# Even heads: block transposes and the value branch inside the inverse; odd heads: a split state update and an earlier product

## The chip, the cores and the metric

One core of one Trainium2 chip runs one program for the whole inference step. The metric is the device time of one execution in microseconds (us); lower is better. The kernel before has 1951.6 us as the median of three runs.

## The reference

One step of a two-layer decoder trunk over 512 prompt tokens and 8 x 8 sample tokens, model width 1024, all in float32. The two layers differ in their mixer; each is followed by a SwiGLU feed-forward block.

```python
def run_trunk(x, conv_a_prev, conv_qkv_prev, delta_prev, ret_prev, pos, w):
...
        h = rmsnorm(x, w['norm_mix'][i])
        if i % 2 == 0:
            y, ca, cq, s = even_mixer(...)   # short conv + gated delta rule, 4 heads of 128
        else:
            y, r = odd_mixer(...)            # retention, 8 heads, qk 128, v 256
        x = x + y.astype(x.dtype)
        h = rmsnorm(x, w['norm_ffn'][i])
        f = (jax.nn.silu(h @ w['ffn_w_gate'][i]) * (h @ w['ffn_w_up'][i])) @ w['ffn_w_down'][i]
        x = x + f.astype(x.dtype)
...
# even mixer, per head
    a_mat = jnp.eye(c, dtype=F32) + jnp.einsum('bnhid,bnhjd->bnhij', kb, kc) * decay * strict
    u_base = lax.linalg.triangular_solve(a_mat, vb, left_side=True, lower=True, unit_diagonal=True)
...
# odd mixer, per head: the state kept for the samples
        r = r * cdec + jnp.einsum('bhck,bhcv->bhkv', k_ * kdec, v_)
```

## The kernel before

All activations live in SBUF transposed (features on the 128 partitions, 512 + 64 = 576 tokens along the free axis). Every weight product is a **unit**: a 128-column slice of a weight over all 1024 rows, 512 KB, loaded by SyncE (`load`, L426) into one of four `raw` slots, split by ScalarE into a high part (`split_hi`, L440) and by GpSimd, in four instructions, into a low part (`split_lo`, L449, instructions at L455), and multiplied on TensorE as high x high, high x low and low x high (`unit`, L466; 48 matmuls of 288 columns). A load waits until the unit three before it has been split, a split until the unit two before it has been multiplied. Two PSUM accumulators alternate; `mx`, four PSUM banks, is for the small products of a head. Each engine runs its own hand-ordered program; numbered steps on one semaphore per engine (`Steps`, tables `E_*` and `O_*`) tie them together.

**Even heads** (three in a loop, a fourth written out). TensorE (`even_tensor`, L1492) puts pieces of units between the small products. In order: unit 0, the norm of k (l2k), three quarters of unit 1, k times k (kk), the norm of q (l2q), the rest of unit 1, the transposes of k (tk), k times q (kq), the transposes of v (tv), P1, and then for s = 2, 4, ..., 64 two eighths of a unit, P_s (`level_p`, L1521), two eighths of a unit, Q_s (`level_q`, L1536). These levels invert the unit triangular 128 x 128 matrices of the four chunks by doubling the size of the inverted diagonal blocks. The inverse `zi` and its transpose `xi` are both kept: P_s is the masked matrix times zi; ScalarE copies it to `pp` (`copy_p`, L1090); Q_s consists of xi times pp (bank 2) and pp times xi (bank 3), with two 64 x 64 products for the samples at s <= 4; VectorE subtracts both banks from zi (z_s) and xi (x_s) (`inverse_step`, L1341). P_(2s) waits for x_s, which VectorE does after z_s. After P64 and Q64 comes the recurrence over the four chunks (u0, S0, ...), on TensorE still mixed with eighths of the next head's k and q units.

VectorE (`even_vector`, L1252) does the four-tap convolutions of k, q and v (`conv_qkv`, L1260), in that order, before it scales k to kT; later vb, the beta-scaled v, straight after the copy kd. During levels 16 to 32 it does the gated convolution of the first mixer (L1357 to L1371). ScalarE (`even_scalar`, L1082) has silu of k, q and v, the squares, the inverse norms (Ln then Exp), and table loads between the silu set and the Ln/Exp set. GpSimd makes the masks b_s and scaled copies.

**Odd heads** (seven in a loop, an eighth written out). Units 0 to 3 are values and gates, 4 and 5 the next head's k and q; then `rows_unit` (L494) multiplies the head's output by two units of the output weight, eight products that each `add_to_x` (L594) adds to x. Near the end TensorE does the variance sums, the last eighth of unit 4, `kvs` (eight states' updates into all four banks of `mx`), unit 5, the rows units. VectorE updates the eight 128 x 256 states `r_s` in one instruction (step rs, L862) once kvs is done, before the first add; between the adds it turns the next head's k and q (`turn_step`, L783). SyncE, at the end of a head's loads, waits for rs and loads the next head's decay constants `ch` (`head_decays`, L1018); then come the next head's units 0 and 1, a wait until ScalarE's DMAs of r_s have ended, the load of the next r_s, unit 2 and so on. ScalarE waits for rs before it sends r_s out and splits the next head's unit 0.

## Time and profile before

| | us |
|---|---|
| median of three runs | 1951.6 |
| lowest and highest of them | 1938.78, 1952.1 |
| the profiled execution's own time | 1946.06 |
| its span, first to last instruction | 1944.3 |
| TensorE busy in the span | 1840.1 |
| mean granted TensorE clock | 0.977 |

The profile is of one execution. Matmuls are pipelined, so that busy time of TensorE is no measure of its peak; the times at which its instructions start, and what they waited for, are what is read below. A granted clock of 1.0 is 2.4 GHz, 0.5 is 1.2 GHz. "x10" means that ten like instructions are merged in a row; a bracket tells how long the engine was idle before the row and what released it.

### The profile page before, as it was taken

The numbers are of one execution on the slowest core, as the hardware profiler recorded it, in microseconds if no ns is written. First come the engines' busy times: TensorE is split into PE (matmuls) and PEld (weight loads), VectorE is DVE, ScalarE is ACT, GpSimd is POOL, SyncE is SP. The second block draws the span as 40 slices with busy tenths as digits, with TensorE's granted clock in tenths as the row PEclk, the third lists the DMA queues.
The fourth block names the chain that finished last, engine by engine and source line by source line (L and its number), as shares of the span: only waits on it lengthen the run. The fifth ranks groups of instructions, "written<-read, shape, count | busy, mean of one in ns | idle before, by whom it ended". The sixth has DMA issues, their size and how long they took to land.

```text
span 1944.3 us, 33917 instructions
## 1 busy us (share of the span) xinstructions
PE 1840.1 (95%) x13431; PEld 1768.5 (91%) x13431; DVE 589.2 (30%) x883; ACT 618.9 (32%) x846; POOL 850.3 (44%) x1061
## 2 busy tenths in 40 slices
PE   6899998998899999999899999999987999999997
PEld 5898888987799999999899999999986999999996
DVE  2636354444311111000452354245425111111002
ACT  3625243342322222112433243334334222222112
POOL 2534435343545445446533443344334444544443
PEclk9999999998999999999899999999998999999998
DMA  5112121211222222223331432243231222222221
GB/s 147 44 34 77 34 75 43 69 42 34 59 86 76 86 78 84 79 78 91 93 106 52 136 115 86 72 125 115 76 94 57 78 84 86 76 86 75 85 81 57
DMA packets 254285, 153.24 MB, mean 79 GB/s; under 512 B 5136, under 2 KB 246549, under 8 KB 254240
## 3 DMA queue, kind: packets, MB, share of 16 engines
q1 hardware_dynamic: 239582, 139.85, 25.1%
q10 hardware_dynamic: 14658, 12.79, 2.0%
q8 instruction: 29, 0.48, 0.1%
q14 instruction: 16, 0.13, 0.0%
HBM read 138.26 MB, written 14.36 MB: 78 GB/s over the span
## 4 chain that ended last, share of the span: by engine, by line
PE 62%; issue 17%; POOL 10%; DVE 6%; ACT 3%; DMA 1%; DVEq 0%; POOLq 0%; ACTq 0%; SPq 0%
PE acc L463 46%; POOL w_lo L455 9%; PE acc L483 7%; PE mx L1494 6%; DVE n_xf L585 1%; PE mx L526 1%; DVE ca L1267 1%; PE mx L875 1%; DMA x_in<-in_x_sample 1%; PE acc L1649 0%; ACT L534 0%; DVE qT L1316 0%; POOL xn_lo L569 0%; ACT std L1085 0%; DVE yT L585 0%
## 5 line engine op out<-in xcount | busy, mean ns | idle before, releaser
L455 POOL TENSOR_TENSOR w_lo<-raw,w_hi 128x256 fp32r<-128x256 f32 x932 | 712.1, 795 | 972.8 <-ACT w_hi L447 972.8
L463 PE MATMUL acc<-xn_hi,w_hi 128*128 128x288 f32 x2224 | 497.8, 305 | 7.6 <-POOL w_lo L455 6.3
L463 PE MATMUL acc<-xn_hi,w_lo 128*128 128x288 f32 x2224 | 477.5, 296 | 0.0
L463 PE MATMUL acc<-xn_lo,w_hi 128*128 128x288 f32 x2224 | 476.4, 296 | 0.0
L447 ACT ACTIVATE w_hi<-raw 128x1024 fp32r<-128x1024 f32 (+1 forms) x237 | 246.9, 1043 | 523.2 <-PE acc L463 475.8
L463 PEld LDWEIGHTS acc<-xn_hi,w_hi 128*128 128x128 f32 x2224 | 357.9, 189 | 23.4 <-issue 16.4
L463 PEld LDWEIGHTS acc<-xn_lo,w_hi 128*128 128x128 f32 x2224 | 359.0, 189 | 0.0
L463 PEld LDWEIGHTS acc<-xn_hi,w_lo 128*128 128x128 f32 x2224 | 358.6, 189 | 0.0
L599 DVE TENSOR_TENSOR x<-acc,x 128x576 f32<-128x576 f32 (+1 forms) x112 | 84.7, 756 | 314.7 <-PE acc L463 312.5
L691 DVE TENSOR_TENSOR f_h<-acc,f_g 128x576 f32<-128x576 f32 x44 | 33.3, 758 | 444.8 <-PE acc L463 444.8
L463 PE MATMUL acc<-h_lo,w_hi 128*128 128x288 f32 x704 | 150.8, 295 | 0.0
L463 PE MATMUL acc<-h_hi,w_hi 128*128 128x288 f32 x704 | 150.8, 295 | 0.0
L463 PE MATMUL acc<-h_hi,w_lo 128*128 128x288 f32 x704 | 150.7, 295 | 0.0
L463 PEld LDWEIGHTS acc<-h_lo,w_hi 128*128 128x128 f32 x704 | 113.7, 188 | 0.0
L463 PEld LDWEIGHTS acc<-h_hi,w_hi 128*128 128x128 f32 x704 | 113.7, 188 | 0.0
L463 PEld LDWEIGHTS acc<-h_hi,w_lo 128*128 128x128 f32 x704 | 113.7, 188 | 0.0
L483 PE MATMUL acc<-xn_hi,w_hi 128*128 128x288 f32 x416 | 92.9, 306 | 13.0 <-ACT xn_hi L555 13.0
L483 PE MATMUL acc<-xn_lo,w_hi 128*128 128x288 f32 x416 | 93.8, 308 | 6.5 <-POOL xn_lo L569 5.5
L658 ACT ACTIVATE f_g<-acc 128x576 f32<-128x576 f32 x44 | 28.7, 651 | 202.8 <-PE acc L463 105.6
L483 PE MATMUL acc<-xn_hi,w_lo 128*128 128x288 f32 x416 | 92.4, 305 | 0.0
L483 PEld LDWEIGHTS acc<-xn_hi,w_hi 128*128 128x128 f32 x416 | 70.1, 198 | 14.7 <-issue 14.7
L483 PEld LDWEIGHTS acc<-xn_lo,w_hi 128*128 128x128 f32 x416 | 69.4, 196 | 10.5 <-POOL xn_lo L569 8.1
(325 smaller groups left out, 2179.6 us busy)
## 6 DMA issues: line engine op xcount, KB each, us to landing
raw<-in_odd_w_in SPq DMA_DIRECT2D x48, 512.0 KB, 4.0
raw<-in_ffn_w_gate SPq DMA_DIRECT2D x44, 512.0 KB, 3.7
raw<-in_ffn_w_up SPq DMA_DIRECT2D x44, 512.0 KB, 3.8
raw<-in_ffn_w_down SPq DMA_DIRECT2D x32, 512.0 KB, 3.7
raw<-in_even_w_in SPq DMA_DIRECT2D x29, 512.0 KB, 3.9
r_s<-in_state_ret SPq DMA_DIRECT2D x8, 1024.0 KB, 6.3
raw<-in_odd_w_out SPq DMA_DIRECT2D x16, 512.0 KB, 3.7
out<-r_s ACTq DMA_DIRECT2D x8, 1024.0 KB, 6.0
```

The costliest lines, as they stand in the source:

```text
L447: nc.scalar.activation(w_hi[:, d, 0:n * P], raw[:, s, 0:n * P], ACT.Copy).then_inc(hi_ready, 1)
L455: ins = nc.gpsimd.tensor_tensor(w_lo[:, d, piece], raw[:, s, piece], w_hi[:, d, piece].bitcast(F32), ALU.subtract)
L463: ins = nc.tensor.matmul(out, w, mv[:, tokens], start=first and n == 0, stop=last and n == 2)
L483: ins = nc.tensor.matmul(out, w, mv[:, k, tokens], start=k == 0 and n == 0, stop=k == KT - 1 and n == 2)
L526: ins = nc.tensor.matmul(mx[:, h, 0:HALF], ones, n_sq[:, t % 2, h * HALF:(h + 1) * HALF], start=t == 0, stop=t == KT - 1)
L585: nc.vector.scalar_tensor_tensor(out=dst, in0=x[:, t, :], scalar=g, in1=n_rs[:, :], op0=ALU.mult, op1=ALU.mult).then_inc(y_norm if last el ...
L599: nc.vector.tensor_tensor(dst, pair_view(p), dst, ALU.add).then_inc(drained[p], 1)
L658: nc.scalar.activation(f_g[:, :], pair_view(0), ACT.Silu).then_inc(drained[0], 1)
L691: nc.vector.tensor_tensor(f_h[:, :], pair_view(1), f_g[:, :], ALU.mult).then_inc(drained[1], 1)
L875: return nc.tensor.matmul(out, lhs, rhs, start=start, stop=stop)
L1267: step(nc.vector.scalar_tensor_tensor(out=b[:, 0:NQ], in0=cbuf[:, t:t + NQ], scalar=w(3 * t + kind), in1=a[:, 0:NQ], op0=ALU.mult, op1=ALU ...
L1494: return nc.tensor.matmul(out, lhs, rhs, start=start, stop=stop)
```

## The change

In the even heads: at levels s = 2 to 16 xi is no longer computed by a product and a subtraction but by VectorE's transpose of 32 x 32 blocks of zi; at these levels zi consists of diagonal blocks of at most 32 x 32. P_(2s) now waits for z_s, Q_(2s) for x_s. The value convolution is cut in two: the first half after inverse_step(2), the second after inverse_step(4). Silu of v comes after copy_p(8), the transposes tv before P16, vb after inverse_step(16), and Q32 waits for vb. ScalarE's return to the Ln/Exp set moves from before copy_p(2) to after the split that follows copy_p(64).

In the odd heads: rs becomes rs0 and rs1, two halves, the first before the first add to x and the second before the third; ScalarE waits for rs1. Unit 5 is multiplied before kvs instead of behind it. The k turn steps stand beside adds 3 to 5, those of q behind the last add. SyncE loads `ch` of a head in that head, behind its unit 1 and the wait for r_s's DMAs, just ahead of the load of r_s, and no longer waits for rs; the first head's `ch` comes this way too and not from ScalarE.

The step tables are reordered to match. The diff, cut to its core:

```diff
-            o_dve.wait(act, h, "rs")
+            o_dve.wait(act, h, "rs1")
...
-            step(nc.vector.scalar_tensor_tensor(out=r_s[:, :, :].rearrange("p b n -> p (b n)"),
-                                                in0=r_s[:, :, :].rearrange("p b n -> p (b n)"), scalar=cdec_s,
-                                                in1=mx[:, :, :].rearrange("p a n -> p (a n)"), op0=ALU.mult,
-                                                op1=ALU.add), "rs")
             for m in range(KT):
+                if m in (0, 2):
+                    half = slice(m // 2 * NB // 2, (m // 2 + 1) * NB // 2)
+                    old = r_s[:, half, :].rearrange("p b n -> p (b n)")
+                    step(nc.vector.scalar_tensor_tensor(out=old, in0=old, scalar=cdec_s,
+                                                        in1=mx[:, m:m + 2, :].rearrange("p a n -> p (a n)"),
+                                                        op0=ALU.mult, op1=ALU.add), f"rs{m // 2}")
                 add_to_x(dve, phase, i, PLAIN[phase] + m, m)
-                if m < 6 and not last:
-                    if m % 3 == 0:
-                        emptied(dve, phase, i, 4 + m // 3)
-                    turn_step(dve, h + 1, m)
+                if 3 <= m < 6 and not last:
+                    if m == 3:
+                        emptied(dve, phase, i, 4)
+                    turn_step(dve, h + 1, m - 3)
+            if not last:
+                emptied(dve, phase, i, 5)
+                for n in range(3, 6):
+                    turn_step(dve, h + 1, n)
...
                 U(4, 7, 8)
+            if not last:
+                U(5)
             o_pool.wait(pe, h, "kdm")
             o_act.wait(pe, h, "oln")
...
             o_pe.done(ins, "kvs")
-            if not last:
-                U(5)
...
                         sp.wait_ge(ret_free, 32 * h + 1)
+                        head_decays(h)
                         sp.dma_start(r_s[:, :, :], state_ret[0].rearrange("b h k v -> h k b v")[ds(h, 1)]
...
-                if not last:
-                    o_dve.wait(sp, h, "rs")
-                    head_decays(h + 1)
...
-            e_dve.wait(act, h, "cv")
-            e_act.done(nc.scalar.activation(vs[:, :], vs[:, :], ACT.Silu), "vs")
             load_table(LN_EXP)
...
             ahead(split_hi, act, phase, i, 3)
-            load_table(LN_EXP)
             copy_p(2)
             copy_p(4)
...
             copy_p(8)
+            e_dve.wait(act, h, "cv")
+            e_act.done(nc.scalar.activation(vs[:, :], vs[:, :], ACT.Silu), "vs")
             copy_p(16)
             ahead(split_hi, act, phase, i, 5)
             copy_p(32)
...
                 ahead(split_hi, act, phase, i, 6)
+            load_table(LN_EXP)
             emptied(act, phase, i, 4)
...
-            act.dma_start(ch[:, :], c_heads[0]).then_inc(s_ch, 16)
...
+            def conv_first(cbuf, kind, name):
...
+                conv_tap(cbuf, kind, name, 1, ca1, ca2)
+
+            def conv_tap(cbuf, kind, name, t, a, b):
+                step(nc.vector.scalar_tensor_tensor(out=b[:, 0:NQ], in0=cbuf[:, t:t + NQ], scalar=w(3 * t + kind),
+                                                    in1=a[:, 0:NQ], op0=ALU.mult, op1=ALU.add), f"{name}{t}")
+
+            def conv_last(cbuf, kind, name, cs):
+                conv_tap(cbuf, kind, name, 2, ca2, ca1)
...
+            def conv_qkv(cbuf, kind, name):
+                conv_first(cbuf, kind, name)
+                conv_last(cbuf, kind, name, cs)
...
             conv_qkv(cbq, 0, "cq")
-            emptied(dve, phase, i, 0)
-            conv_qkv(cbuf, 2, "cv", cs=vs)
-
             e_act.wait(dve, h, "k_inv")
             step(nc.vector.tensor_tensor(kT[:, :], ks[:, :], std[:, :], ALU.mult), "kT")
...
                                          kdec[0:TS, NC, ds(h, 1)].to_broadcast([TS, P]), ALU.mult), "kd")
-            e_pe.wait(dve, h, "tv")
-            nc.vector.tensor_tensor(vb[:, 0:NC, :], chunks(mx[:, 2, :]), beta_of(0, NC, P), ALU.mult)
-            step(nc.vector.tensor_tensor(vb[0:TS, NC, :], mx[0:TS, 3, 0:P], beta_of_sample(P), ALU.mult), "vb")
-
...
                 if s <= 4:
                     nc.vector.tensor_tensor(zi[0:TS, TP:T], zi[0:TS, TP:T], mx[0:TS, 1, TS:2 * TS], ALU.subtract)
-                    nc.vector.tensor_tensor(xi[0:TS, TP:T], xi[0:TS, TP:T], mx[0:TS, 1, 2 * TS:3 * TS], ALU.subtract)
                 e_dve.done(nc.vector.tensor_tensor(zi[:, 0:TP], zi[:, 0:TP], mx[:, 2, :], ALU.subtract), f"z{s}")
-                if s < MASKS[-1]:
+                if s <= SQUARE // 2:
+                    e_dve.wait(dve, h, f"z{s}")
+                    if s <= 2:
+                        nc.vector.transpose(xi[0:TS, TP:T], zi[0:TS, TP:T])
+                    e_dve.done(nc.vector.transpose(xi[:, 0:TP], zi[:, 0:TP]), f"x{s}")
+                elif s < MASKS[-1]:
                     e_dve.done(nc.vector.tensor_tensor(xi[:, 0:TP], xi[:, 0:TP], mx[:, 3, :], ALU.subtract), f"x{s}")
                 e_dve.wait(dve, h, f"x{s}" if s < MASKS[-1] else f"z{s}")
 
-            for s in (2, 4, 8, 16):
-                inverse_step(s)
+            inverse_step(2)
+            emptied(dve, phase, i, 0)
+            conv_first(cbuf, 2, "cv")
+            inverse_step(4)
+            conv_last(cbuf, 2, "cv", vs)
+            inverse_step(8)
+            inverse_step(16)
+            e_pe.wait(dve, h, "tv")
+            nc.vector.tensor_tensor(vb[:, 0:NC, :], chunks(mx[:, 3, :]), beta_of(0, NC, P), ALU.mult)
+            step(nc.vector.tensor_tensor(vb[0:TS, NC, :], mx[0:TS, 1, 0:P], beta_of_sample(P), ALU.mult), "vb")
...
-                e_dve.wait(pe, h, f"x{s // 2}")
+                e_dve.wait(pe, h, f"z{s // 2}")
                 ins = by_chunk(0, lambda c: bm[:, b, c * P:(c + 1) * P], lambda c: at(zi, c))
...
             def level_q(s):
                 e_act.wait(pe, h, f"p{s}")
-                if s == 2:
+                e_dve.wait(pe, h, f"x{s // 2}")
+                if s == 32:
                     e_dve.wait(pe, h, "vb")
                 ins = by_chunk(2, lambda c: at(xi, c), lambda c: at(pp, c))
-                if s < MASKS[-1]:
+                if SQUARE // 2 < s < MASKS[-1]:
                     ins = by_chunk(3, lambda c: at(pp, c), lambda c: at(xi, c))
                 if s <= 4:
-                    mm(mx[0:TS, 1, TS:2 * TS], xi[0:TS, TP:T], pp[0:TS, TP:T])
-                    ins = mm(mx[0:TS, 1, 2 * TS:3 * TS], pp[0:TS, TP:T], xi[0:TS, TP:T])
+                    ins = mm(mx[0:TS, 1, TS:2 * TS], xi[0:TS, TP:T], pp[0:TS, TP:T])
                 e_pe.done(ins, f"Q{s}")
...
-            e_act.wait(pe, h, "vs")
-            e_dve.wait(pe, h, "aqk")
-            for c in range(NC):
-                nc.tensor.transpose(mx[:, 2, c * P:(c + 1) * P], at(vs, c), ident)
-            e_pe.done(nc.tensor.transpose(mx[0:TS, 3, 0:P], vs[:, TP:T], ident), "tv")
...
             for j, pair in ((2, (2, 4)), (3, (8, 16)), (4, (32, 64))):
                 for t, s in enumerate(pair):
                     U(j, 4 * t, 4 * t + 2)
+                    if s == 16:
+                        e_act.wait(pe, h, "vs")
+                        for c in range(NC):
+                            nc.tensor.transpose(mx[:, 3, c * P:(c + 1) * P], at(vs, c), ident)
+                        e_pe.done(nc.tensor.transpose(mx[0:TS, 1, 0:P], vs[:, TP:T], ident), "tv")
                     level_p(s)
                     U(j, 4 * t + 2, 4 * t + 4)
                     level_q(s)
```

## Rows read from the trace of the kernel before

**Rows 1.** Busy time by stretch: an even head, an odd head (PE, PEld, DVE, ACT, POOL, PEclk).
```profile
182.50:288.20 105.70, 98.29 (x726) 91.56 (x725) 53.13 (x96) 40.93 (x61) 45.15 (x54) 0.98 0.20 55
...
1158.00:1224.00 66.00, 64.85 (x496) 62.22 (x495) 27.46 (x38) 23.92 (x35) 26.20 (x33) 1.00 0.35 100
```

**Rows 2.** Timeline of TensorE in the second even head: start, duration, instructions.
```profile
188.41 2.46 PE L1494 MATMUL mx<-kT 128*128 128x128 f32 x10 [3.17 <-DVE kT L1308]
...
190.79 1.76 PE L1494 MATMUL mx<-sq,every 128*128 128x288 f32 x4
...
195.74 1.42 PE L1494 MATMUL mx<-qT,kT 128*64 128x64 f32 x10 [1.05 <-DVE qT L1316]
...
198.17 0.66 PE L1577 MATMUL mx<-every,vs 128*128 128x128 f32 x4 [1.01 <-DVE dt L1321]
...
199.26 0.66 PE L1527 MATMUL mx<-every,bm 128*128 128x128 f32 x4 [0.33 <-DVE kd L1325]
...
202.61 1.41 PE L1494 MATMUL mx<-zi,bm 128*128 128x128 f32 x10 [0.66 <-DVE xi L1338]
```

**Rows 3.** The same in the first and the last even head: the product kq.
```profile
87.58 1.42 PE L1494 MATMUL mx<-qT,kT 128*64 128x64 f32 x10 [2.17 <-DVE qT L1316]
...
405.27 1.42 PE L1494 MATMUL mx<-qT,kT 128*64 128x64 f32 x10 [0.57 <-DVE qT L1316]
```

**Rows 4.** Windows with the granted clock (after POOL's column), first and second even head.
```profile
92.00:96.00 4.00, 4.00 (x18) 3.73 (x17) 1.80 (x6) 0.00 (x0) 1.87 (x3) 0.50 0.46 128
...
189.00:190.00 1.00, 1.00 (x6) 1.00 (x6) 1.00 (x2) 1.00 (x1) 1.00 (x2) 0.50 0.00 0
...
198.00:200.00 2.00, 1.51 (x11) 1.07 (x11) 1.67 (x5) 0.34 (x1) 2.00 (x4) 1.00 0.00 0
```

**Rows 5.** Timeline of ScalarE in the second even head.
```profile
182.70 0.69 ACT L1088 ACTIVATE std<-std 128x576 f32<-128x576 f32 x1
...
187.51 0.68 ACT L1124 ACTIVATE sq<-qs 128x576 f32<-128x576 f32 x1
...
188.78 1.28 ACT L534 ACT_TABLE_LOAD   x1
```

**Rows 6.** Timeline of VectorE there: the end of q's convolution, and kT.
```profile
182.32 0.28 DVE L1272 SCALAR_TENSOR_TENSOR cs<-cbq,pw,ca 128x64 f32<-128x64 f32 x1
...
187.25 1.10 DVE L1308 TENSOR_TENSOR kT<-ks,std 128x576 f32<-128x576 f32 x1
```

**Rows 7.** Timeline of TensorE there: Q2, into bank 2, into bank 3, the samples' last.
```profile
205.63 1.05 PE L1494 MATMUL mx<-pp,xi 128*128 128x128 f32 x8
...
206.52 1.06 PE L1494 MATMUL mx<-xi,pp 128*128 128x128 f32 x8
...
207.68 0.28 PE L1494 MATMUL mx<-xi,pp 64*64 64x64 f32 x2
```

**Rows 8.** Timeline of VectorE there: vb, x16, z32.
```profile
199.32 0.69 DVE L1328 TENSOR_TENSOR vb<-mx,bh 128x512 f32<-128x512 f32 x1
...
227.65 0.68 DVE L1348 TENSOR_TENSOR xi<-xi,mx 128x512 f32<-128x512 f32 x1
...
232.98 0.69 DVE L1346 TENSOR_TENSOR zi<-zi,mx 128x512 f32<-128x512 f32 x1
```

**Rows 9.** The chain that ended last, in order of time: one unit of 48 matmuls.
```profile
530.40 6.40 PE acc L483 x48
```

**Rows 10.** Timeline of all engines at the end of an odd head.
```profile
1201.65 2.35 DVE L862 SCALAR_TENSOR_TENSOR r_s<-r_s,ch,mx 128x2048 f32<-128x2048 f32 x1
...
1202.95 0.52 PE L463 MATMUL acc<-oyh,w_hi 128*128 128x288 f32 x2 [0.39 <-POOL w_lo L455]
...
1204.17 0.35 SPq L1019 DMA_DIRECT2D ch<-const_heads  x1
...
1210.72 0.37 SPq L1026 DMA_DIRECT2D r_s<-in_state_ret  x1
...
1212.36 1.06 ACT L447 ACTIVATE w_hi<-raw 128x1024 fp32r<-128x1024 f32 x1 [6.71 <-DMA raw<-in_odd_w_in]
...
1216.96 0.53 PE L463 MATMUL acc<-xn_hi,w_hi 128*128 128x288 f32 x2 [0.73 <-POOL w_lo L455]
```

More of the change, by code:

```diff
@@ L161 @@
 MASKS = (1, 2, 4, 8, 16, 32, 64)
+SQUARE = 32
 SPREAD = P // 4
@@ L217 @@
 A_DVE = ("zero", "gate", "sum", "ad", "relu", "softplus", "neg", "g", "gc0", "gc")
-E_PE = ("rows", "l2k", "kk", "l2q", "tk", "kq", "tv", "P1", *(f"{a}{s}" for s in _LATER for a in "PQ"),
+E_PE = ("rows", "l2k", "kk", "l2q", "tk", "kq", "P1", "P2", "Q2", "P4", "Q4", "P8", "Q8", "tv", "P16", "Q16",
+        "P32", "Q32", "P64", "Q64",
         "u0", "Rs", "S0", "o0", "R1", "u1", "S1", "o1", "R2", "u2", "us", "S2", "o2", "R3", "u3", "S3", "o3",
         "os", "onorm", "Ss")
-E_ACT = ("gr", "eg", "ks", "k_sq", "dt_lo", "dm_lo", "k_ln", "k_inv", "dm", "dt", "qs", "q_sq", "vs", "q_ln", "q_inv",
-         *(f"p{s}" for s in _LATER), "yah", "uu0", "uu1", "uu2", "us_", "uu3", "o_sq", "o_ln", "o_inv", "ybh")
+E_ACT = ("gr", "eg", "ks", "k_sq", "dt_lo", "dm_lo", "k_ln", "k_inv", "dm", "dt", "qs", "q_sq", "q_ln", "q_inv",
+         "p2", "p4", "p8", "vs", "p16", "p32", "p64", "yah", "uu0", "uu1", "uu2", "us_", "uu3", "o_sq", "o_ln", "o_inv", "ybh")
 E_DVE = ("pw", "gate", "pre_k", "ck0", "ck1", "ck2", "ck", "pre_v", "bg", "pre_q",
-         "cq0", "cq1", "cq2", "cq", "cv0", "cv1", "cv2", "cv", "kT", "dmb", "A", "qT",
-         "aqk", "kd", "vb", *(f"{a}{s}" for s in (1, 2, 4, 8, 16) for a in "zx"),
[2 rows of a table added]
          "ca0", "ca1", "ca2", "z32", "x32", "z64", "s0", "rr1", "rs", "s1", "rr2", "s2", "rr3", "s3", "yal",
@@ L231 @@
 O_DVE = ("qg", "att", "r0", "r1", "r2", "r3", "of_p", "of_s", "o_both", "cen", "sq_both",
-         "on0", "y0", "on1", "y1", "yl0", "yl1", "rs")
+         "on0", "y0", "on1", "y1", "yl0", "yl1", "rs0", "rs1")
 ROTARY = ("tk", "rk", "tq", "rq")
@@ L1258, in step @@
                 e_dve.wait(dve, h, name)
-            def conv_qkv(cbuf, kind, name, cs=cs):
+            def conv_first(cbuf, kind, name):
                 nc.vector.tensor_copy(out_q[:, kind, ds(h, 1), 0:3].rearrange("p a n -> p (a n)"), cbuf[:, SQ - 3:SQ])
@@ L1265, in conv_qkv @@
                 step(nc.vector.tensor_scalar(ca1[:, 0:NQ], cbuf[:, 0:NQ], w(kind), None, ALU.mult), name + "0")
-                for t, (a, b) in ((1, (ca1, ca2)), (2, (ca2, ca1))):
-                    step(nc.vector.scalar_tensor_tensor(out=b[:, 0:NQ], in0=cbuf[:, t:t + NQ], scalar=w(3 * t + kind),
-                                                        in1=a[:, 0:NQ], op0=ALU.mult, op1=ALU.add),
-                         f"{name}{t}")
+                conv_tap(cbuf, kind, name, 1, ca1, ca2)
[4 more added lines that the diff above has]
+                conv_tap(cbuf, kind, name, 2, ca2, ca1)
                 nc.vector.scalar_tensor_tensor(out=cs[:, 0:TP], in0=cbuf[:, 3:3 + TP], scalar=w(9 + kind),
```

2 rows, old and new, of the table E_DVE are left out of this document.

## Prediction

> **What bounds the kernel now.** I read four views. First the busy time by stretch: in an even head TensorE is busy 98.3 of 105.7 us, in an odd head 64.9 of 66.0 [rows 1]. One unit of 48 matmuls takes 6.40 us [rows 9], so a quarter of a unit, the filler between P and Q, takes 1.6. TensorE is the bound nearly everywhere; only work taken from it and waits taken from it can count. Then the timeline of TensorE in the second even head. It waits 3.17 us for kT, 1.05 for qT, 1.01 for the masked kq, 0.33 for kd and 0.66 for x1, all between l2k and P2, 6.2 us in sum [rows 2]; from P2 to Q64 there is no bracket, so the levels are bound by TensorE itself. Third the granted clock: behind the long wait it is 0.50, i.e. 1.2 GHz [rows 4], and kk takes 2.46 us where the like product kq takes 1.42 [rows 2]. Fourth the end of an odd head: TensorE waits twice for a low part of weights, and before the second, ScalarE waited 6.71 us for a weight load that SyncE issued only after its wait for r_s [rows 10].
>
> **Levels 2 to 16.** Removed from TensorE in each: the product into xi, eight matmuls, 0.89 us by the distance of the starts of Q2's two products [rows 7]. Four levels give 3.56; the two sample products (0.28 as shown, about 0.16 each in the pipeline) 0.32; together 3.9 per even head, all on the path. In place of a subtraction of 0.68 [rows 8] VectorE gets a transpose that no row shows. Lower bound 0.5, upper 1.5: the shape moves as many elements as the 0.68 subtraction, and kT, from SBUF to SBUF beside GpSimd's traffic, took 1.10 for 576 [rows 6]. I take 0.7. It runs behind z_s while TensorE does a quarter unit, P, and a quarter unit (about 4.2 us), against z_s 0.8 plus 0.7, so x_s costs nothing. The two halves of the value convolution lie there too: the whole takes from 182.6 to 187.25, 4.6 us [rows 6], about 2 and 2.6 in halves; 0.8 + 0.7 + 2.6 = 4.1 of a round of 5. Without that cover each us over would be a us per level.
>
> The Trainium skill (Vector Engine (DVE) Microarchitecture Reference, The reshape front-end and per-opcode configuration) has this transpose at one element per cycle and lane, and VectorE: DVE Perf Modes (The three transpose paths) says that only 32 x 32 blocks turn on their own, which would end the trick at level 16 as the kernel does. By its rate 512 elements take 0.53 us and a fixed part; the sum would be the same.
>
> **tv and vb moved.** tv (the start of P1 would be some 0.9 us behind it) stood in the shadow of the wait for kd: 198.17 to 199.26, P1 waiting 0.33 more [rows 2]. Before P16 it has no shadow: +0.9 per head. vb, 0.69 and a sample part of 0.27, about 1.1 with its waits [rows 8], leaves the stretch before z1 and comes behind x16. There VectorE is full: x16 ends at 228.33, and the gated convolution keeps it until z32 at 232.98 [rows 8]. z32 starts 1.2 late; z32's 0.7 under a quarter unit of 1.6 leaves 0.8; P64 waits 0.4 per head. The table load of 1.28 [rows 5] that now stands ahead of the first uu lies mostly in idle time of ScalarE; between 0 and 1.28 I take 0.2.
>
> Levels to recurrence: 3.9 - 0.9 - 0.4 - 0.2 = 2.4 per head, 9.6 for four; 0.2 more as the last head has slack for the table load: 9.8.
>
> **From l2k to P2.** In the second head k's inverse norm ends at 182.70 + 0.69 = 183.4 [rows 5], q's convolution before it [rows 6]. kT can end at 184.4 instead of 188.35; unit 1's pieces end at 185.1, so kk starts then, 3.3 earlier, at full clock. What is late next is ScalarE: the square of q ends at 187.51 + 0.68 = 188.2 [rows 5], so l2q waits 1.8. Without silu of v the table load starts 0.7 earlier, at 188.1, ends at 189.4; Ln 0.75 and Exp 0.69 end at 190.9; qT, 0.8 to 1.5, at about 192.2; kq at 192.3 instead of 195.74. P1 follows kq by 3.52 [rows 2], held by kd as before, at 195.8, with a wait of 2.3 behind kq that tv filled in part. P2 followed P1 by 3.35 [rows 2]; without vb and without x1 in its wait it is 2.55 (0.85 for P1, 1.6 for the pieces, 0.1): 198.35 instead of 202.61. That is 4.3, also for the third head. In the first, kq waited 2.17 at full clock after a shorter wait for kT [rows 3]; kq gains only 1.8, but P2 had run late at half clock [rows 4]: 3.7. In the last, kq waited 0.57 [rows 3]: 2.1. Sum 14.4.
>
> **What the clock takes back.** The one long wait goes, but new ones come close together: 1.8 (l2q), about 1 (kq), 2.3 (P1), over 5 us of 10. In the first head waits of 2.17 and 1.01 with one product between them [rows 3] were followed by the half clock from 90 to 96 [rows 4]; in the second, waits of 1.05 and 1.01 left it at 1.00 [rows 2, 4]. Mine are nearest to the first head's. A fall costs half its length on busy time, 1.5 to 3 us as such stretches lasted 3 to 6 us; I take 2.4 per head, 9.6 in all. So l2k to P2 brings 14.4 - 9.6 = 4.8, and the even heads 14.6.
>
> **Odd heads.** SyncE no longer waits for rs (until 1204.17 [rows 10]); unit 0 of the next head is asked for when its slot is free, some 10 us earlier, and not beside the 1 MB of r_s going out. Its split then waits only for the first rows unit (about 1209.5), so the low part is done by 1213.7 and the wait at 1216.96, 0.73 as shown and 0.88 by the starts [rows 10], is gone. The rows units' own start waits for a low part (0.39 [rows 10]) that hangs on unit 4; that stays, and swallows most of the 0.2 that kvs waited for the Ln. I take 1.03 per head boundary, seven of them: 7.2. The costs: rs, 2.35 whole [rows 10], now starts behind the later kvs; its second half follows add 1 and ends about 1208.3, 4.3 later. r_s's DMA goes out then; SyncE came 6.5 us after rs to the next r_s [rows 10], so `ch`, r_s and unit 2 are asked for at about 1215. `ch` is first needed by the mask of att, at 1216 + 6.4 = 1222.5, unit 2's split at about 1223.5. Both covers are 1 to 5 us wide. The add that frees unit 0's accumulator keeps its time, about 1215.8, since three turn steps still precede it.
>
> **The sum.** 14.6 + 7.2 = 21.8 from the profiled execution's own 1946.1 (1944.3 span and 1.8 around it) gives 1924.3. That execution lies 5.5 below the median of the runs; against the median it is 1951.6 - 21.8 = 1929.8.
>
> **The rivals.** (B) The clock does not fall in the even heads. For it: no single new wait reaches the 3.17 that preceded the fall, and the second head stood two short ones. Against: the first head. It gives back 9.6: 1920.2. The Trainium skill (TensorE: Matmul & The Clock Gate, Why this matters for your kernels) warns of long idle gaps between bursts; by that rule B would come, and the first head's rows speak against it.
> (C) VectorE is the new bound inside the levels: a transpose at 1.5 and the value convolution stretched by GpSimd as kT's 1.10 was. P64 waits 1.2 instead of 0.4, z8 about 0.5, and the clock falls a second time at the l2q wait, 1.2 more: 2.5 per head, 10: 1939.8.
> (D) The odd boundary keeps its wait, since ScalarE's split of unit 0 now stands behind rs1 or the loads bunched at 1215 make unit 2 late: 7.2 lost: 1937.0.
> (E) Slower: the clock stays low from l2q through the levels. Some 20 us of busy TensorE at half speed cost 10 per head, 40 in all against 21.8 + 9.6: 1960. It decides from about 16 us of half clock per head; the longest stretch seen is 6.
>
> **How the numbers follow.** Forecast 0.50, B 0.17, C 0.20, D 0.10, E 0.03. The forecast's own bounds (fall cost 1.5 to 3, P64's wait 0 to 1, spread of the runs) are 1923 to 1936. The range reaches from below B, since runs of before reach down to 1939, to above C: 1914 to 1942. A change of 1% (19.5 us) is what a measurement of this kernel can tell from none: B and most of the forecast (0.78 of it) and a little of the rest are beyond it, 0.58; the remaining forecast, C and D are within, 0.39; slower 0.03.
>
> **What would show it.** The windows: even heads near 101.5 us (105.7), odd boundaries 65.0 (66.0), clock 0.5 for 3 to 6 us around P1. TensorE: no bracket at kk, a wait of about 1.8 at l2q and 2.3 at P1, 0.4 at P64, none at the next unit 0. VectorE: transposes of about 0.7. I would be wrong by a transpose over 2 us, a clock that stays up, or SyncE's later loads reaching TensorE.

## The result and the profile after

The changed kernel takes 1917.3 us (median of four runs, 1914.4 to 1922.3) and the kernel before, measured beside it, 1945.9 (1938.8 to 1952.1): a ratio of 0.9857, with an interval of 0.9807 to 0.9906. That is 28.6 us, or 1.4%. The forecast was 1929.8, with a range of 1914 to 1942, so the sign is right and the gain is larger than forecast. The forecast had taken its 21.8 us off a median of 1951.6, that of three runs; the fourth lowers it to 1945.9. Of the 12.5 us between forecast and result 5.7 are therefore the base, and 6.8 the gain. The profiled executions differ by more: 1912.6 us of span against 1944.3, 31.7 us, and this section accounts for those.

First the windows of the changed kernel: one even head, one odd head, the place where the clock falls, and the wait behind kq that follows it (columns: length, then PE, PEld, DVE, ACT, POOL busy, the granted clock, DMA share, GB/s).

```profile
182.50:281.80 99.30, 93.88 (x689) 87.70 (x688) 51.32 (x94) 40.98 (x60) 44.56 (x55) 0.98 0.22 59
...
1129.23:1194.05 64.82, 64.19 (x495) 62.10 (x494) 28.65 (x39) 23.82 (x34) 26.26 (x33) 1.00 0.34 102
...
181.00:185.00 4.00, 4.00 (x17) 3.61 (x17) 1.03 (x1) 3.47 (x4) 3.79 (x5) 0.57 0.47 131
...
187.00:189.10 2.10, 0.03 (x1) 0.00 (x0) 1.69 (x4) 0.00 (x0) 2.10 (x4) 1.00 0.00 0
```

An even head is now 99.3 us long, where it was 105.7 [rows 1], and TensorE waits 5.4 us of it instead of 7.4. An odd head is 64.8 instead of 66.0. The clock is at its lower level (0.50, 1.2 GHz) for about 3.5 us between l2k and P2 of each even head (3.5 to 7 before), but the place is another. Then TensorE's timeline in the second even head, which answers to [rows 2]:

```profile
177.57 1.31 PE L1511 MATMUL mx<-kT 128*128 128x128 f32 x10
180.75 1.61 PE L1511 MATMUL mx<-sq,every 128*128 128x288 f32 x4 [1.86 <-ACT sq L1130]
...
184.98 0.60 PE L1586 MATMUL mx<-every,kT 128*128 128x128 f32 x4
185.41 0.27 PE L1587 MATMUL mx<-every,kT 128*64 128x128 f32 x1
185.62 1.42 PE L1511 MATMUL mx<-qT,kT 128*64 128x64 f32 x10
189.13 0.66 PE L1544 MATMUL mx<-every,bm 128*128 128x128 f32 x4 [2.09 <-DVE kd L1335]
...
191.81 1.41 PE L1511 MATMUL mx<-zi,bm 128*128 128x128 f32 x10
```

The product kk (first line) has no wait and runs at full speed, 1.31 us where it took 2.46. The first long wait is now 1.86 us for q's square ahead of l2q; behind it the clock falls and comes back at about 185 us, just ahead of kq. kq shows no wait. P1 (the line with L1544) waits 2.09 for kd, and the clock stays at 1.00 behind that. Further down the head the levels themselves show two brackets of 0.15 us:

```profile
208.55 0.60 PE L1598 MATMUL mx<-every,vs 128*128 128x128 f32 x4
208.99 0.27 PE L1599 MATMUL mx<-every,vs 128*64 128x128 f32 x1
209.10 1.06 PE L1511 MATMUL mx<-zi,bm 128*128 128x128 f32 x8
...
220.22 1.16 PE L1511 MATMUL mx<-zi,bm 128*128 128x128 f32 x8 [0.15 <-DVE zi L1350]
...
226.28 0.49 PE L1511 MATMUL mx<-uu,kd 128*128 128x128 f32 x2 [0.15 <-ACT uu L1160]
```

The first two lines are tv in its new place ahead of P16: the next product starts 0.55 us after it. The fourth is P64, and the last one a product of the recurrence behind the first uu. VectorE between two levels, with the new transposes:

```profile
196.19 0.21 DVE L1349 TENSOR_TENSOR zi<-zi,mx 64x64 f32<-64x64 f32 x1 [3.83 <-PE mx L1511]
196.32 0.67 DVE L1350 TENSOR_TENSOR zi<-zi,mx 128x512 f32<-128x512 f32 x1
197.03 0.24 DVE L1354 STREAM_TRANSPOSE xi<-zi 64x64 f32<-64x64 f32 x1
197.20 0.66 DVE L1355 STREAM_TRANSPOSE xi<-zi 128x512 f32<-128x512 f32 x1
```

The transpose of 128 x 512 takes 0.66 us here and 0.71 at levels 4, 8 and 16, about as long as the subtraction that it replaces (0.68, [rows 8]).

Last the end of an odd head, TensorE, then SyncE, then ScalarE's split of unit 0's weights, which answer to [rows 10]:

```profile
1172.85 1.15 PE L883 MATMUL mx<-vtok,kdm 32*128 32x256 f32 x16
1174.62 0.53 PE L465 MATMUL acc<-oyh,w_hi 128*128 128x288 f32 x2 [0.62 <-POOL w_lo L457]
...
1187.56 0.53 PE L465 MATMUL acc<-xn_hi,w_hi 128*128 128x288 f32 x2
```

```profile
1174.65 0.37 SPq L434 DMA_DIRECT2D raw<-in_odd_w_in  x1
1185.20 0.35 SPq L1027 DMA_DIRECT2D ch<-const_heads  x1
1185.73 0.37 SPq L1035 DMA_DIRECT2D r_s<-in_state_ret  x1
```

```profile
1181.45 1.06 ACT L449 ACTIVATE w_hi<-raw 128x1024 fp32r<-128x1024 f32 x1 [5.44 <-PE acc L465]
```

Unit 0's load was issued at 1174.65, ahead of the head's own `ch` and r_s. ScalarE's split of it waits for TensorE to leave the buffer, no longer for a DMA, and at 1187.56 unit 0 of the next head starts without the 0.73 us wait. The wait at the first rows unit is still there, 0.62 where it was 0.39.

Put in order of time, the positions of the same product in both traces give this account. Each stretch runs from the start of one product to the start of another; the third row adds the first two.

| stretch | before | after | gain | forecast |
|---|---|---|---|---|
| start to P2 of the first head | 95.60 | 92.50 | 3.1 | |
| u0 to the next head's P2, three times | 70.55, 69.45, 67.37 | 66.39, 66.70, 65.89 | 8.4 | |
| the two together (l2k to P2 alone: 11.1) | | | 11.5 | 4.8 |
| P2 to u0, four times | 36.46, 36.21, 36.22, 36.74 | 32.92, 32.91, 32.90, 32.77 | 14.1 | 9.8 with the recurrence |
| last u0 to the end of the even stage | 40.76 | 42.21 | -1.4 | |
| to the first odd head | 470.27 | 469.74 | 0.5 | |
| seven odd boundaries | 461.11 | 453.61 | 7.5 | 7.2 |
| last odd head and the rest | | | -0.5 | 0 |
| sum | | | 31.7 | 21.8 |

### The profile page after: what moved, and what is told of

It reads as the page before. It is cut to its first block, busy times and chain, and to the rows that moved or that the text cites. A ratio compares the mean times of both kernels' runs of the same rounds, so it can differ in the third digit from the quotient of the medians.

```text
span 1912.6 us, 33665 instructions
## 1 busy us (share of the span) xinstructions
PE 1816.6 (95%) x13287; PEld 1751.6 (92%) x13287; DVE 592.2 (31%) x887; ACT 619.5 (32%) x846; POOL 849.4 (44%) x1061
## 4 chain that ended last, share of the span: by engine, by line
PE 49%; issue 15%; POOL 10%; DVE 3%; ACT 1%; DMA 0%; POOLq 0%; ACTq 0%; DVEq 0%
PE acc L465 40%; POOL w_lo L457 9%; PE acc L485 7%; PE mx L1511 1%; DVE n_xf L587 1%; PE mx L883 1%; PE mx L528 0%; POOL n_ss L565 0%; POOL xn_lo L571 0%; DVE yT L587 0%; DMA out<-y_out 0%; DVE xn_lo L571 0%; POOL kdm L980 0%; DVE y_out L1506 0%; PE mx L524 0%
```

## The experiments

"Before" was measured again in each of the three series on which the experiments ran: 1953.7, 1951.2 and 1949.4 us. Each ratio below is against the one of its own series.

| kernel | median us | ratio to before | interval |
|---|---|---|---|
| e1 odd part alone | 1942.0 | 0.9940 | 0.9921 to 0.9959 |
| e2 block transposes alone | 1931.4 | 0.9889 | 0.9872 to 0.9906 |
| e3 value convolution moved alone | 1944.4 | 0.9951 | 0.9932 to 0.9970 |
| e4 changed, kd ahead of aqk | 1905.3 | 0.9757 | 0.9735 to 0.9780 |
| e5 changed kernel again | 1917.2 | 0.9831 | 0.9793 to 0.9869 |
| e6 changed, transposes twice | 1923.2 | 0.9863 | 0.9828 to 0.9897 |
| e7 changed, unit 1's piece earlier | 1927.9 | 0.9884 | 0.9849 to 0.9919 |
| e8 e4 and e7 together | 1912.3 | 0.9806 | 0.9770 to 0.9842 |
| e9 changed, filler ahead of l2q | 1927.4 | 0.9899 | 0.9874 to 0.9923 |
| e10 e4 with fillers | 1905.1 | 0.9791 | 0.9764 to 0.9818 |
| e11 e4, unit 2's split later | 1900.2 | 0.9759 | 0.9735 to 0.9783 |
| e12 before, SyncE's wait alone | 1945.7 | 0.9990 | 0.9974 to 1.0006 |

### The three parts by themselves

e1 is the kernel before with the hunks of the change in the odd heads and in SyncE's order; e2 has only the hunks of the inverse; e3 has the hunks that move the value convolution, silu of v, tv and vb, with the inverse as before. Since bank 3 is still used by each Q there, vb stands ahead of inverse_step(16) in e3, and tv waits for x8.

> The kernel before with only the odd heads' edits. Theory 1 (the parts add up, each takes its own waits from TensorE): the even heads as before, the distance of two odd heads 64.8 us instead of 66.0, 7 x 1.18 = 8 us less by the middle of the run and about 6.7 less at the end, since the last head gave 1.5 back; about 1938 against a span of 1944.3. Rival 1a (the odd heads only gained because the even heads had become earlier or the loads had shifted): no change.

> The kernel before with only the block transposes: levels 2 to 16 without the product into xi, P waiting for z, Q for x; the value convolution, tv and vb stay where they were. Theory 1: TensorE has 0.89 us less in each of four levels and 0.3 in the samples' parts, 3.9 per even head, 15.5 in all; besides P2 no longer waits for x1, up to 0.6 per head more: 15 to 18 us less. The kT wait of 3.2 and the half clock behind it stay. Rival 1b (the levels are bound by VectorE's chain of a subtraction and a transpose, or by ScalarE's copy, as soon as the product is gone): brackets appear at P and Q, and it gives less than 8.

> The kernel before with only the value branch moved: convolution halves behind levels 2 and 4, silu behind P8's copy, tv ahead of P16, vb ahead of level 16's subtraction (bank 3 is still used by each Q, so vb must come there), the table load moved; xi still by products. Theory 1: l2k to P2 gets shorter by what the changed kernel showed, 3.2, 3.3, about 3 and 1.7 us, tv costs 0.9 per head in the levels, z16 comes 1.1 later behind vb and P32 may wait for about 1: 11 - 4 - 3 = 4 to 8 us less in all. Rival 1c (the moves by themselves give nothing, since tv used a shadow and vb now stands in the levels, and only together with the shorter levels do they pay): within 2 us of before.

The core of each, e1, e2, e3:

```diff
-            o_dve.wait(act, h, "rs")
+            o_dve.wait(act, h, "rs1")
...
             if not last:
                 U(4, 7, 8)
+            if not last:
+                U(5)
...
-                if not last:
-                    o_dve.wait(sp, h, "rs")
-                    head_decays(h + 1)
```

```diff
-                    nc.vector.tensor_tensor(xi[0:TS, TP:T], xi[0:TS, TP:T], mx[0:TS, 1, 2 * TS:3 * TS], ALU.subtract)
...
-                if s < MASKS[-1]:
+                if s <= SQUARE // 2:
+                    e_dve.wait(dve, h, f"z{s}")
...
+                    e_dve.done(nc.vector.transpose(xi[:, 0:TP], zi[:, 0:TP]), f"x{s}")
...
-                if s < MASKS[-1]:
+                if SQUARE // 2 < s < MASKS[-1]:
                     ins = by_chunk(3, lambda c: at(pp, c), lambda c: at(xi, c))
```

```diff
-            emptied(dve, phase, i, 0)
-            conv_qkv(cbuf, 2, "cv", cs=vs)
...
+            inverse_step(2)
+            emptied(dve, phase, i, 0)
+            conv_first(cbuf, 2, "cv")
+            inverse_step(4)
+            conv_last(cbuf, 2, "cv", vs)
```

In e1 the seven boundaries take 453.66 us, 7.45 less than before, which is all of the change's gain in the odd heads. In e2 P2 to u0 takes 32.73, 32.37, 32.39 and 32.52, together 15.6 less; but u0 to the next P2 grew by 2.6 over three heads, and the windows show eight stretches of half clock up to the last u0 instead of five. In e3 the first P2 comes 0.6 earlier, u0 to the next P2 is 5.7 shorter over three heads, and P2 to u0 is 2.7 longer. The ratios of the parts leave 0.60, 1.11 and 0.49%, in sum 2.2%, where the whole gave 1.7% (e5) and 1.4%; with intervals of some 0.2% on each part and 0.4% on the whole this doesn't show that they overlap. By position it comes out the other way: the last u0 comes 14.8 us earlier in e2, 3.7 in e3 and 25.6 in the changed kernel. Some 6 of the 7 us that the two parts lack are places of the clock's fall: at P1 in three heads of e3, where it costs more (below), and behind each recurrence in e2. The inverse is the largest part by either account.

The distances between the starts of products in the second even head show how the levels divide:

| | P2-P4 | P4-P8 | P8-P16 | P16-P32 | P32-P64 | P64-u0 | sum |
|---|---|---|---|---|---|---|---|
| before | 6.97 | 6.98 | 5.95 | 5.92 | 5.90 | 4.49 | 36.21 |
| e2 | 5.95 | 5.84 | 4.96 | 4.96 | 6.17 | 4.49 | 32.37 |
| changed | 5.95 | 5.84 | 5.50 | 4.95 | 6.17 | 4.50 | 32.91 |

The four levels give 4.1 us in e2. In the changed kernel tv takes back 0.54 between P8 and P16. The 0.27 that P32 to P64 lost is P64's start behind z32, and it is there in e2 too, where vb was not moved. Its cause is GpSimd. In e2 VectorE's small copy into out_a, ahead of z32, took 1.06 us and ended with GpSimd's mask:

```profile
220.16 1.06 DVE L1368 COPY out_a<-bufa 128x2 f32 x1
```

```profile
219.92 1.28 POOL L1730 TENSOR_TENSOR bm<-dm,ce 128x512 f32<-128x512 f32 x1
```

The copy took 0.38 before and 0.37 in the changed kernel, and there too it ended within 0.03 of the mask; z32 starts 2.50 to 2.52 behind the mask's end in the first three heads of all three. In the changed kernel vb fills time that e2 spends in that copy, so that moving it cost nothing at P64.

### Transposes twice

```diff
+                    nc.vector.transpose(sq[:, 0:TP], zi[:, 0:TP])
                     e_dve.done(nc.vector.transpose(xi[:, 0:TP], zi[:, 0:TP]), f"x{s}")
```

> The changed kernel with each of the four big transposes per head done once more, into a spare tile, ahead of the real one: 0.7 us more on VectorE at levels 2, 4, 8 and 16, nothing else. Theory 3 (x is covered by the quarter unit, P and the next quarter unit, and VectorE has slack everywhere but ahead of z32): P, Q at levels 4 to 32 start as before, only P64 waits 0.15 + 0.7 = 0.85 instead of 0.15 (z32 0.7 later): 0.7 per head, 2.8 us in all. Rival 3a (VectorE's chain is the bound of the levels): 0.7 per level, 2.8 per head, 11 us in all. Rival 3b (slack everywhere): nothing.

P2 to u0 became 34.21, 34.24, 34.29 and 32.81, so 1.3 to 1.4 us more in three heads and nothing in the last. Of it 1.2 to 1.4 is at P64, as TensorE's timeline of e6 shows:

```profile
223.95 1.16 PE L1512 MATMUL mx<-zi,bm 128*128 128x128 f32 x8 [1.33 <-DVE zi L1350]
```

So at levels 2 to 8 VectorE has over 0.7 us of room, and behind level 16 it has none: the place was as expected, but the size expected was 0.7. The other half in this head is VectorE's copy into bufa, 0.96 us where it took 0.33, which now ends with GpSimd's mask. The profiles of e6 and e5 differ by 3.8 us, which is what P64 took in three heads; the medians differ by 6.0, and 2.8 was expected. A transpose of 1.5 us, as in rival C, would have cost at P64 about what this one did. It measured 0.66 to 0.71, and the rival fell with it.

### The wait for kd

```diff
+            e_pe.wait(dve, h, "tk")
+            nc.vector.tensor_tensor(kd[:, 0:NC, :], chunks(mx[:, 0, :]),
...
             e_pe.wait(dve, h, "kq")
             e_pool.wait(dve, h, "dtm")
             nc.vector.tensor_tensor(dt_[:, 0:TP], mx[:, 2, :], dt_[:, 0:TP], ALU.mult)
...
-            e_pe.wait(dve, h, "tk")
-            nc.vector.tensor_tensor(kd[:, 0:NC, :], chunks(mx[:, 0, :]),
```

kd needs only tk, which is done before kq, yet it stood behind the product of kq with the decays.

> The changed kernel with one more move: VectorE makes kd ahead of aqk. kd needs only tk, which is done before kq; P1 waits only for kd. Theory 2 (the 2.1 us wait ahead of P1 is VectorE's order, and it lies on the path): the wait goes, P1 starts behind kq, then P2 is held by z1 behind aqk and starts some 1.5 to 2.1 earlier per head: 6 to 8 us less than the changed kernel. Rival 2a (what is saved ahead of P1 is waited for at P2, since z1 still stands behind aqk): under 2 us. Rival 2b: TensorE is fuller ahead of P1, and the clock falls elsewhere or not at all; the granted clock tells.

e4 takes 1905.3 us, 12 less than the changed kernel by the medians; l2k to P2 is shorter by 9.6 in the four heads, where 6 to 8 was expected. TensorE in its second even head:

```profile
177.26 1.24 PE L1511 MATMUL mx<-sq,every 128*128 128x288 f32 x4 [1.86 <-ACT sq L1130]
...
181.99 1.42 PE L1511 MATMUL mx<-qT,kT 128*64 128x64 f32 x10 [1.36 <-DVE qT L1326]
183.24 0.60 PE L1544 MATMUL mx<-every,bm 128*128 128x128 f32 x4
...
185.90 1.41 PE L1511 MATMUL mx<-zi,bm 128*128 128x128 f32 x10
```

P1 follows kq with no wait; kq to P2 takes 3.91 us where it took 6.19. Over three heads u0 to the next P2 falls from 199.0 to 192.8. The rows show one thing more: the same wait of 1.86 ahead of l2q, and this time the clock stays up behind it (1.24 against 1.61 us for l2q). In this kernel it fell at l2q in the first and third heads and once behind a recurrence (at 234.5 us), and in the second and fourth heads it did not fall at l2q.

### Where the clock falls, and what that costs

e5 is the changed kernel, once more.

> The changed kernel itself, beside the runs below, so that they can be compared on one chip. Both theories: the marks of every head as in its first profile (kq 13.7 us and P2 19.8 us behind the first head's l2k, odd heads 64.8 apart); a span within 5 us of 1912.6.

Its median is 1917.2, like the first. Its profile has six stretches of half clock up to the last u0, not four: in the second, third and fourth head at l2q again, but in the first head at P1 (89.5 to 93.5), and two more (192 to 195.5 behind P2, and 243 to 247). So where the clock falls is no fixed property of this kernel. Up to P1 e6 has the same work on every engine; over the twelve heads of the two profiles and e6 the clock fell at l2q in nine, and in the other three, with the same wait ahead of l2q, it fell at P1. That gives prices for the same work at both levels: P1 to P2 takes 4.02 us in e5's first head and 2.54 in that of the first profile, 1.5 more; P2 to Q2 takes 3.94 against 3.03, 0.9 more; and l2q to kq takes 4.87 in the changed kernel and 4.73 in e4, 0.14 more. A fall at l2q is nearly free, one at P1 is not: l2k to P2 took 1.3 to 1.7 us longer in the three heads that had it there.

e7 tries to remove the fall at l2q by putting a quarter of unit 1 into the wait ahead of it, e8 does so on top of e4, and e9 and e10 put in extra products whose results nothing uses.

```diff
+            U(1, 6, 8)
             e_act.wait(pe, h, "q_sq")
             squares(2, "l2q")
-            U(1, 6, 8)
```

> The changed kernel with the last quarter of unit 1 multiplied ahead of the norm product l2q instead of behind it, in the time in which TensorE waits for the square of q. Theory 4 (the half clock at l2q comes from that wait of 1.86 us, and its cost is on the path): the wait shrinks to 0.25, l2q and the transposes run at full clock, ScalarE's Ln starts 0.3 to 0.8 us earlier, kq 0.9 earlier (it then waits for qT): 3 to 4 us less in all, if the clock does not fall at the wait that now stands ahead of kq. Rival 4a (waits only change places: about 2.5 us of waiting now comes in one piece ahead of kq, the clock falls there and P1, P2 run slow): the same time within 2 us or up to 4 us more.

> Both moves: kd ahead of aqk and unit 1's last quarter ahead of l2q. Theory 2 with 4: 8 to 10 us (kd) and 3 to 4 us less than the changed kernel, about 12. Rival 4a: as kd first alone, 10 less, or a little worse.

```diff
             e_pe.done(mm(mx[0:TS, 1, 0:TS], kT[:, TP:T], kT[:, TP:T]), "kk")
+            by_chunk(2, lambda c: at(kT, c), lambda c: at(kT, c))
+            by_chunk(3, lambda c: at(kT, c), lambda c: at(kT, c))
```

> The changed kernel with 16 products of 128 columns added (k transposed against itself, into two banks that are free then, results unused; about 1.8 us of work), put into TensorE's wait of 1.86 us ahead of each head's l2q. Nothing else moves. Theory 5 (the fall of the clock at l2q, which the changed kernel shows in all four heads for 3.4 us, costs about 1 us a head, since l2q and the decays' products run at half speed): the granted clock stays at 1.00 through 181 to 185 us of the second head, P2 comes about 1 us earlier in each head, span 3 to 4 us below the changed kernel, time about 1913. Rival 5a (the chain from l2q on runs through ScalarE and VectorE, and the half clock is hidden, or the clock then falls at the next wait, P1's 2.09 us): P2 is where it was, time 1917 or up to 3 us more.

> The kernel with kd ahead of aqk on VectorE, with the same 16 added products ahead of l2q and 8 more between q_ln and kq (results unused). If the half clock at l2q costs about 1 us a head here as well (theory 5): P2 at 16.5 us of its head instead of 17.5, time 1901 to 1902. Rival 5a: 1905 again, or more, if the eight products ahead of kq hold it up.

None brought what the theory asked for. The rivals had the mechanism, and e10's had the time too; but they allowed at most 4 us more for e7, 3 for e9 and a little for e8, and it was far more. e7 is 10.7 us slower than the changed kernel of its series, e9 10.2 slower than the changed kernel's two medians, e8 7 slower than e4, and e10 the same as e4. TensorE in e9's second even head:

```profile
183.47 1.24 PE L1511 MATMUL mx<-sq,every 128*128 128x288 f32 x4
...
188.19 1.42 PE L1511 MATMUL mx<-qT,kT 128*64 128x64 f32 x10 [1.35 <-DVE qT L1326]
191.71 1.12 PE L1544 MATMUL mx<-every,bm 128*128 128x128 f32 x4 [2.10 <-DVE kd L1335]
...
196.20 1.89 PE L1511 MATMUL mx<-zi,bm 128*128 128x128 f32 x10
```

The wait ahead of l2q is gone and l2q runs at full clock, 1.24 us. But a wait of 1.35 has come up at kq, and behind P1's 2.10 the clock falls, from 190.5 to 197.5: P1 to P2 takes 4.49 us instead of 2.68, and P1 to P4 10.92 instead of 8.63. e7 has the same with 2.94 at kq and low clock from 188 to 198. Both have further low stretches of about 3.5 us behind the recurrences, three in e9 and two in e7. By position e9 is 13.3 us behind the changed kernel's first profile: 8.9 between l2k and u0, 3.2 behind the recurrences, the rest outside the heads. In e10, where there is no long wait left between kk and P2, the clock fell only behind two recurrences (before the last head's), and the time is that of e4. So half of the reasoning behind these runs was wrong: the fall at l2q could be removed, but there was nothing to win by it, and where another long wait stood behind it, the fall came there at its full price.

### What sets kq

That filling and half clock leave kq where it is asks what kq waits for. kk to kq takes 8.05 us in the changed kernel, and 7.90, 7.90, 7.89 and 7.91 in e4, e7, e9 and e10. kq waits for qT on VectorE (in the changed kernel qT ends first, and TensorE, slowed at l2q, comes 0.15 later), and the length of that one instruction is 1.05 to 1.84 us over these kernels. Next to it stands GpSimd's second mask. VectorE and GpSimd of the changed kernel:

```profile
183.97 1.44 DVE L1326 SCALAR_TENSOR_TENSOR qT<-qs,std 128x576 f32<-128x576 f32 x1 [4.23 <-ACT std L1094]
```

```profile
177.49 2.78 POOL L457 TENSOR_TENSOR w_lo<-raw,w_hi 128x256 fp32r<-128x256 f32 x4 [7.78 <-ACT w_hi L449]
...
183.52 1.27 POOL L1742 TENSOR_TENSOR bm<-dm,ce 128x512 f32<-128x512 f32 x1
```

The mask ends at 184.79 and qT at 185.41, 0.62 later. In the other kernels the two ends are 195.06 and 195.68 (before), 181.31 and 181.94 (e4), 187.51 and 188.13 (e7), 187.52 and 188.14 (e9), 182.09 and 182.71 (e10), 179.22 and 179.84 (e11): 0.62 or 0.63 in all seven. The other heads and profiles say the same: 0.61 or 0.62 in all 56 even heads of the fourteen, with qT between 0.77 and 2.63 us long. When both overlap, qT ends a fixed time behind the mask, whenever it began. GpSimd works without a break from 177.49, so kq hangs on a chain that begins with the low half of unit 2's weights (2.78 us), and TensorE's clock at l2q has no part in it. The Trainium skill (SBUF — State Buffer, SBUF: two separate sides) says that VectorE and GpSimd share a pair of ports that the one which came first holds for its whole instruction; qT's ends agree with that. In the first head of the kernel before, qT began at 84.90, under an earlier mask, and still ended 0.62 behind one that began only at 85.65: there, by these ends, VectorE did not get its turn between two of GpSimd's instructions.

```diff
-            ahead(split_hi, act, phase, i, 2)
             e_act.done(nc.scalar.activation(dt_[:, :], dt_[:, :], ACT.Exp, scale=-1.0), "dt")
...
             inverse_root("q", 2, 1.0)
+            ahead(split_hi, act, phase, i, 2)
...
-            ahead(split_lo, pool, phase, i, 2)
             e_act.wait(pool, h, "dt")
...
             mask(2)
+            ahead(split_lo, pool, phase, i, 2)
```

> The kernel with kd ahead of aqk, with the high half of the weights of unit 2 rounded on ScalarE behind q's root instead of between k's transposed product and q's square, and its low half on GpSimd behind the mask of level 2. Theory 6 (l2q's wait of 1.86 us is the delay of ScalarE's square by that rounding, 1.04 us of it): l2q, qT and kq come about 1 us earlier in each head, P2 at about 16.5 us, time about 1901. Rival 6a: ScalarE or GpSimd are then late for unit 2, whose weights TensorE needs in the inverse, or the square isn't what is late: time 1905 or more.

e11 takes 1900.2 us (1898.9 to 1901.0), e10 beside it 1905.1 (1903.7 to 1909.6). TensorE, then VectorE and GpSimd of its second head:

```profile
175.95 1.24 PE L1511 MATMUL mx<-sq,every 128*128 128x288 f32 x4 [0.91 <-ACT sq L1129]
...
179.89 1.42 PE L1511 MATMUL mx<-qT,kT 128*64 128x64 f32 x10 [0.58 <-DVE qT L1326]
...
182.69 0.52 PE L465 MATMUL acc<-xn_hi,w_hi 128*128 128x288 f32 x2 [0.69 <-POOL w_lo L457]
184.37 1.31 PE L1511 MATMUL mx<-zi,bm 128*128 128x128 f32 x10
```

```profile
178.79 1.05 DVE L1326 SCALAR_TENSOR_TENSOR qT<-qs,std 128x576 f32<-128x576 f32 x1 [2.72 <-ACT std L1094]
```

```profile
177.94 1.28 POOL L1742 TENSOR_TENSOR bm<-dm,ce 128x512 f32<-128x512 f32 x1
179.78 6.20 POOL L457 TENSOR_TENSOR w_lo<-raw,w_hi 128x256 fp32r<-128x256 f32 x8 [0.56 <-ACT w_hi L449]
```

kk to kq takes 6.17 instead of 7.90, 1.7 less, more than the 1.04 of ScalarE that was expected: the 2.78 us of w_lo left GpSimd's queue as well, and qT took 1.05. Unit 2's weights are now late by 0.69, which takes part of it back; over three heads u0 to the next P2 is 4.7 us shorter than in e4. In none of its four heads did the clock fall between kk and u0. e11 computes all that the reference asks, and is the fastest kernel of this study.

### The odd heads

e12 is the kernel before, with one part of the change:

```diff
                         sp.wait_ge(ret_free, 32 * h + 1)
+                        head_decays(h)
...
-                if not last:
-                    o_dve.wait(sp, h, "rs")
-                    head_decays(h + 1)
```

> The kernel before, with one part of the change alone: each head's decays are worked out at the head's own start from its own loaded row, and SyncE no longer waits for the row's use before it issues the next loads. Theory 3 (the odd boundaries' gain of 1.18 us is mostly the removed wait of 0.73 to 0.39 us for weights at unit 0 and what follows from it): the odd heads' distance falls from 66.0 to about 65.1, seven times, 6 us, time 1945 against 1951. Rival 3a (the gain needs the head's other moves together): distance stays 66.0, time 1951.

The seven boundaries take 457.8 us, 3.3 less than before, where the whole odd part takes 7.5 off (65.4 a head against 64.8 in e1). The wait at unit 0 is gone. The median is 3.7 lower, and the interval of the ratio reaches from 0.9974 to 1.0006, so no more than that is shown. SyncE's wait is a little under half of the odd gain; the expectation of 6 us was too high. The other 0.6 us a head comes from unit 5 ahead of kvs, the state's update in halves, or both; no run tells them apart.

## Why the prediction came out as it did

**kk and l2q: right.** kk has no wait and the full clock; l2q waits 1.86 where 1.8 was forecast.

**kq: 0.8 late or more in each head.** The forecast had kq 7.2 us behind kk (185.1 and 192.3) and it came 8.05 behind. It took qT for 0.8 to 1.5 us from the end of Exp on. qT did last 1.44, but its end was set by GpSimd's mask, as shown above, and the working didn't look at GpSimd's queue at all. With four heads this is some 3 us, and l2k to P2 brought 11.1 instead of the 14.4 that stood there before the clock's share.

**P1 and P2: right.** P1 came 3.51 behind kq (3.52), its wait was 2.09 (2.3), and P2 followed by 2.68 (2.55).

**What the clock takes back: the step that failed.** The forecast took 2.4 us a head, 9.6 in all, for a fall around P1. The clock did fall once in each even head, for about 3.5 us, in the length forecast, but at l2q. There TensorE had to wait for qT in any case, and the fall cost 0.15 us (8.05 against 7.90 from kk to kq), 0.6 over four heads. At P1 it would have cost 1.5 to 1.8 up to P2, as e5 and e9 show, and in e9, where it lasted 7 us, 2.3 up to P4. So the error was not in whether the clock falls, nor much in the price of a fall at P1, but in taking the fall to be there and its price to be the same anywhere, without asking which wait lies behind it. Rival B gave 1920.2, nearest to the 1917.3 measured, by a mechanism that didn't happen: nine microseconds came back since the fall was hidden, not since it stayed away. That it came at l2q in all four heads of this profile was also luck: in e5 and e6 three heads of eight had it at P1.

**Levels 2 to 16: right in kind, 0.9 a head too low.** Four levels gave 4.1 (3.9 forecast, four times 0.89 and the samples). tv took 0.54 back, not 0.9: the next product started 0.55 behind it. P64 took 0.27, not 0.4; e2 has the same 0.27 from GpSimd's mask alone, so vb added nothing. That leaves 3.3 in P2 to u0 (2.6 forecast); the last head even had 4.0. The first uu took 0.22 (0.2), from the starts of u0 and S0: 1.34 before, 1.56 after.

**The odd heads: right.** 7.5 against 7.2: no wait at unit 0, 64.8 a head for the forecast 65.0, the wait ahead of the rows unit kept. The split of that gain was not right: the removed SyncE wait alone gave 0.5 a head where the forecast saw nearly all.

**Rivals C, D and E.** The transpose measured less than half of the 1.5 that C needed; e6 shows that C's mechanism is real, since P64 would have been the place. The odd boundary did not keep its wait (D). The clock was back before kq in every head (E).

**Not forecast:** the stretch from the last u0 to the end of the even stage grew by 1.4. It is 40.6 to 44.4 us in the fourteen profiles, 44.4 in e1 where the even heads were left alone, so it isn't the change's. It goes with the time that the clock spends at 1.2 GHz in it: 40.6 to 41.1 us where that is 14 us (before, e4, e5), 42.2 where it is 17 (changed, e3, e6, e10), 43.3 at 20.5 (e11), 44.1 to 44.4 at 24 (e1, e7, e9). The sum of the account (31.7) is between two profiled executions; the medians differ by 28.6 and, beside e5, by 34.0. The kernel before spreads over 17 us between executions, so the whole gain is known only to some microseconds.

## What to carry to other kernels

A fall of the clock costs its share only where TensorE sets the pace; before pricing one, see whether a wait for another engine stands behind it. Before filling a wait, ask the same: filling one that covers such a fall moved it to a dearer place, and the kernel took 10 us more. When a VectorE instruction's length changes between heads or kernels, set its end against the end of GpSimd's instruction, and shorten GpSimd's queue ahead of it rather than VectorE's.

## What was unexpected of the hardware

The block transpose on VectorE took 0.66 to 0.71 us for 128 x 512 of 32 bits and 0.24 for 64 x 64, like a subtraction of that size. The Trainium skill (VectorE: DVE Perf Modes, The three transpose paths) has it turn 32 x 32 blocks on their own, which is what the kernel uses it for up to level 16; here it cost about what the subtraction of 0.68 us did.

The same wait of 1.86 us ahead of l2q left the clock at 1.00 in e4's second head and was followed by 0.50 in the changed kernel's. In e11, with waits of 0.91, 0.58 and 0.69, it stayed at 1.00 from kk to u0, as in its other heads. In the kernel before, the fall came behind 3.17 us of waiting in the second and third heads; here 1.81 to 1.86 was enough, and 2.09 ahead of P1 was followed by a fall in e5's first head, two heads of e6, e7 and e9, and not in the changed kernel's first profile, where the clock had come back from its fall at l2q some 4 us before. The Trainium skill (TensorE: Matmul & The Clock Gate, Why this matters for your kernels) warns of long idle gaps between bursts of matmuls; these rows show a fall behind waits of 1.81, 1.86 and 2.09 us. What decides between two like waits stays open.

qT, one instruction over 128 x 576, took between 0.77 and 2.63 us, and ended 0.61 or 0.62 behind GpSimd's mask in all 56 even heads. A copy of 128 x 2 into out_a took 1.06 us in e2 and 0.37 in the changed kernel, and ended within 0.03 of a mask in both.
